# The entry of a transformer block: the first modulation column on TensorE, the root table loaded early, two x tiles scaled by GpSimd

## The chip, the cores and the metric

The kernel runs on one core of a Trainium2 chip. The metric is the device time of one execution in microseconds; the median of three runs of the kernel before is 2016.6 us. The engines of a core are TensorE (PE), VectorE (DVE), ScalarE (ACT), GpSimd (POOL) and SyncE (SP), which here issues nearly all transfers. Each works through its own instructions in order and waits for others on semaphores.

## The reference

One bidirectional encoder block on 512 tokens of 2048 channels. What the change touches is its start:

```
c_act = jax.nn.silu(c)
mod = c_act @ w_ada[l] + b_ada[l]
sh_a, sc_a, gt_a, sh_m, sc_m, gt_m = [m[:, None, :] for m in jnp.split(mod, N_MOD, axis=-1)]
h = rms_norm(x, g_pre_attn[l]) * (1.0 + sc_a) + sh_a
proj = h @ w_in[l]
```

`rms_norm` divides each token by the root of its mean square plus 1e-6 and multiplies by a gain. Then follow two groups of attention heads, an output projection, and a squared-ReLU MLP, all float32.

## The kernel before

**Tiling.** Tokens are in 4 tiles of 128 (`NT`), channels in 16 chunks of 128 (`KD`). Products are made of a high and a low part of each operand, three products each. `x_tok[t]` is a tile of x with tokens on the partitions; `x_t` is x turned, channels on the partitions.

**The entry, per tile t.** ScalarE squares and sums the first 1024 columns (`x_square`, line 843), VectorE the others (line 1514). ScalarE takes the root (`x_root`, line 836), VectorE its reciprocal (line 1520) and scales the tile (`x_scale`, line 1522). TensorE turns the tile in 16 transposes into 4 banks (`turn_x`, line 2369), and ScalarE copies the banks to `x_t` (`x_copies`, line 851).

**Silu and the modulation columns.** silu(c) lies as 16 columns of 128 in `silu_c`. TensorE spreads it over all partitions by 16 transposes into banks 4 to 7 (line 2348, semaphore `spread`), ScalarE copies two of the banks to `silu_b` (line 830), VectorE the other two (line 1475). For chunk n a transposed slice of `w_ada` of 128 x 2048 lands in `w_turned[n % 4]`; `column(n)` on VectorE multiplies it by `silu_b` and sums along the row in one instruction (line 1483), and `column_out(n)` makes of the sum the factor `gsc_a[:, n]` (line 1490). 32 such columns are summed, 16 for the factor and 16 for the shift.

**Heads.** For chunk n ScalarE makes the high part of the weights (`start_w_hi`, line 819) and of h (`start_h`: h_hi and its float32 copy h_f, line 874); VectorE makes the low parts (`start_w_lo`, line 1435; `h_low`, line 1508). TensorE multiplies: chunk 0 in three passes over 7 banks (`first_heads`, lines 2385, 2389, 2393), each later chunk in 21 products (`head_chunk`, lines 2402 to 2404). For n above 4 the low part of h for chunk n - 1 stands on VectorE behind the sum of column n.

**What sets the order.** Each engine's order is written out by hand. SyncE issues gains, ident, bias, x tiles 0 to 2, slice 0, x tile 3, weights 0, and then slice and weights in turn; a buffer is loaded again when its reader has counted up. GpSimd sets `ones` to 1 at the start and has nothing else to do until the end of the 32 columns.

Of the kernel before, what the change touches and what calls it, by code (L numbers as in the profile page):

```python
# [51 lines left out]
X_BANK = (7, 4, 5, 6)  # L52
TURN_BANK = (4, 5, 3, 7)
# [101 lines left out]
def build(nc, a, out, x1_dram, y_dram):  # L155
    with ExitStack() as ctx:
# [29 lines left out]
        scale_b = small("scale_b", [KD])  # L186
        gsc_a = small("gsc_a", [KD])
# [145 lines left out]
        silu_steps, spread, spread_copied = sems("silu_steps spread spread_copied")  # L333
        col_summed, heads_done, heads_out, bias_added = sems("col_summed heads_done heads_out bias_added")

        x_sq, x_var, x_sqrt, x_normed, x_turned, x_t_ready = sems("x_sq x_var x_sqrt x_normed x_turned x_t_ready")
# [475 lines left out]
        def _(act):  # L812
# [15 lines left out]
            for m in range(2):  # L828
                act.wait_ge(spread, m + 1)
                nc.scalar.activation(silu_b[:, m * COLS:(m + 1) * COLS], bank[4 + m][:], ACT.Copy).then_inc(spread_copied, 1)  # L830

            def x_root(t):

                act.wait_ge(x_var, t + 1)
                act.wait_ge(x_sq, t + 1)
                nc.scalar.activation(stat_s[:, t, 0:1], stat[:, t, 0:1], ACT.Sqrt, scale=1.0 / D, bias=stat_v[:, t, 0:1]).then_inc(x_sqrt, 1)

            def x_square(t):

                act.wait_ge(x_landed[t], 16)  # L840
                if t:
                    act.wait_ge(x_sq, t)
                nc.scalar.activation(x_junk[:, 0:HALF], x_tok[t][:, 0:HALF], ACT.Square, accum_out=stat[:, t, 0:1]).then_inc(x_sq, 1)

            def x_copies(t):

                for kk in range(NT):
                    n = NT * t + kk
                    act.wait_ge(x_turned, n + 1)
# [11 lines left out]
            def start_h(n):  # L861

                k = n % KD
                act.wait_ge(cols_ready, n + 1)
                if n >= KD:
                    act.wait_ge(w_used, k + 1)
                else:
                    act.wait_ge(x_t_ready, NT * (NT - 1) + k // 4 + 1)
# [558 lines left out]
        def _(dve):  # L1427
# [45 lines left out]
            for m in (2, 3):  # L1473
                dve.wait_ge(spread, m + 1)
                nc.vector.tensor_copy(silu_b[:, m * COLS:(m + 1) * COLS], bank[4 + m][:]).then_inc(spread_copied, 1)

            def column(n):

                if n == 0:
                    dve.wait_ge(spread_copied, 4)  # L1480
                dve.wait_ge(w_turned_landed[n % RING], 16 * (n // RING + 1))
                w = w_turned[n % RING][:]
                stt(w, w, 1.0, silu_b[:], ALU.mult, ALU.mult, accum_out=col_sum[:, n:n + 1]).then_inc(col_summed, 1)

            def column_out(n):

                k = n % KD
                dve.wait_ge(col_summed, n + 1)
                if n < KD:
                    ts(gsc_a[:, k:k + 1], col_sum[:, n:n + 1], scale_b[:, k:k + 1], gains[:, KD + k:KD + k + 1], ALU.add, ALU.mult).then_inc(cols_ready, 1)  # L1490
                else:
                    tt(shf_a[:, k:k + 1], col_sum[:, n:n + 1], bias[:, k:k + 1], ALU.add).then_inc(cols_ready, 1)
# [17 lines left out]
            def x_square(t):  # L1510

                dve.wait_ge(x_landed[t], 16)
                part_x = x_tok[t][:, HALF:D]
                own.step(stt(x_junk[:, HALF:D], part_x, 1.0, part_x, ALU.mult, ALU.mult, accum_out=stat[:, t, 1:2]))
                ts(stat_v[:, t, 0:1], stat[:, t, 1:2], 1.0 / D, EPS, ALU.mult, ALU.add).then_inc(x_var, 1)

            def x_scale(t):

                dve.wait_ge(x_sqrt, t + 1)
                own.step(nc.vector.reciprocal(rstd[:, t, 0:1], stat_s[:, t, 0:1]))  # L1520
                for cols in (slice(0, COLS), slice(COLS, D)) if t == NT - 1 else (slice(0, D),):
                    ts(x_tok[t][:, cols], x_tok[t][:, cols], rstd[:, t, 0:1], None, ALU.mult).then_inc(x_normed, 1)

            for t in range(NT):
                if t == NT - 1:
                    column(0)
                    column_out(0)
                x_square(t)
                x_scale(t)
            start_w_lo(0)  # L1530
            h_low(0)
            for n in range(1, CHUNKS):
# [3 lines left out]
                column_out(n)  # L1536
                start_w_lo(n)
# [772 lines left out]
        def _(pe):  # L2310
# [31 lines left out]

            pe.wait_ge(const_landed, 32)
            pe.wait_ge(ones_ready, 1)
            pe.wait_ge(silu_steps, 2)
            for k in range(KD):
                b, c = 4 + k // 4, k % 4 * P
                ins = nc.tensor.transpose(bank[b][:, c:c + P], silu_c[:, k:k + 1].broadcast_to([P, P]), ident[:])
                if k % 4 == 3:
                    ins.then_inc(spread, 1)  # L2350

            def turn_x(t):

                for kk in range(NT):
                    n = NT * t + kk
                    if t == NT - 1:
                        b = X_BANK[kk]
                        pe.wait_ge(x_normed, NT + (kk > 0))
                        if kk == 0:
                            pe.wait_ge(spread_copied, 4)  # L2360
                    else:
                        b = kk
                        if t:
                            pe.wait_ge(x_t_ready, n - X_BANKS + 1)
                        else:
                            pe.wait_ge(x_normed, 1)
# [10 lines left out]
            def first_heads():  # L2377
# [3 lines left out]
                for i in range(QH):  # L2381
                    wh, _ = weight_cols(0, i * P)
                    if i >= 4:
                        pe.wait_ge(x_t_ready, KD - NT + i - 2)
# [51 lines left out]
            for t in range(NT):  # L2436
                if t:
                    pe.wait_ge(x_normed, t + 1)
                turn_x(t)
            first_heads()  # L2440
# [676 lines left out]
def packed(a):  # L3117
# [5 lines left out]
    return {"w_ada_t": np.ascontiguousarray(np.concatenate([w_ada[:, SC_A:SC_A + D].T, w_ada[:, SH_A:SH_A + D].T])),  # L3123
# [4 lines left out]
```

## Time and profile before

| what | value |
|---|---|
| median of 3 runs | 2016.6 us (2016.35 to 2017.35) |
| the profiled execution's own time | 2017.13 us |
| its span in the profile | 2015.2 us |
| TensorE busy | 1984.6 us, 98% of the span |
| VectorE busy | 1730.3 us |
| ScalarE busy | 1005.1 us |
| GpSimd busy | 161.3 us |

The profile's times count from the start of the span. The time of an execution is 1.9 us more than its span here. A busy share of a whole run says little about a stage of 50 us; for that one reads the timeline, which lists the instructions in order of time, with the idle time before each in brackets and what ended it.

### The profile page before, as it was taken

To read this page: it belongs to the slowest core of one execution; us is meant where nothing else is said; L and a number is where in the kernel's file an instruction comes from. 1 tells how busy PE (TensorE), PEld (TensorE's weight loads), DVE (VectorE), ACT (ScalarE), POOL (GpSimd) and SP (SyncE) were. 2 spreads that over 40 slices of the span, in tenths; PEclk is the share of its full clock that TensorE was granted. 3 is DMA by queue.
4 is the path that set the end of the run, shared out by engine and by line. 5 is a ranking of instruction groups with operands and counts; after the bars stand their busy time and mean duration, and the time that the engine had idled before them with its cause. 6 is when DMAs were issued, how large, how long until landed. Compare 5 with 4: busy or idle time off the path is not lost.

```text
span 2015.2 us, 30682 instructions
## 1 busy us (share of the span) xinstructions
PE 1984.6 (98%) x11171; PEld 1738.4 (86%) x11171; DVE 1730.3 (86%) x1993; ACT 1005.1 (50%) x1424; POOL 161.3 (8%) x173
## 2 busy tenths in 40 slices
PE   7999999999999999999999999999999999999998
PEld 5887888788888878999999999998888888888886
DVE  7897998788877788999999999988898898898866
ACT  6464223688733374565656565655343343434322
POOL 0000000257400000000000000000300000000000
PEclk9999999999999999999999999999999999999999
DMA  9988768600378746667676766668746546556452
GB/s 357 369 297 293 237 215 233 214 1 21 130 248 261 239 163 188 206 216 230 214 229 213 229 213 229 214 222 331 255 176 250 193 181 250 186 187 252 175 179 84
DMA packets 260180, 432.28 MB, mean 215 GB/s; under 512 B 27648, under 2 KB 155264, under 8 KB 247168
## 3 DMA queue, kind: packets, MB, share of 16 engines
q1 hardware_dynamic: 242576, 361.42, 53.1%
q0 software_dynamic: 15936, 63.97, 8.6%
q10 hardware_dynamic: 1584, 5.77, 0.8%
q8 instruction: 53, 0.87, 0.2%
q14 instruction: 31, 0.25, 0.0%
HBM read 367.15 MB, written 63.96 MB: 214 GB/s over the span
## 4 chain that ended last, share of the span: by engine, by line
PE 91%; DVE 5%; ACT 3%; issue 1%; DMA 0%; POOL 0%; SPq 0%; POOLq 0%; ACTq 0%; DVEq 0%
PE bank L2817 9%; PE bank L2819 9%; PE bank L2818 9%; PE bank L2839 9%; PE bank L2841 9%; PE bank L2840 9%; PE bank L2324 6%; PE bank L2326 6%; PE bank L2325 6%; PE bank L2900 1%; PE bank L2899 1%; PE bank L2898 1%; PE bank L2337 1%; PE bank L2338 1%; PE bank L2339 1%
## 5 line engine op out<-in xcount | busy, mean ns | idle before, releaser
L1367 ACT ACTIVATE hi<-w 128x1024 fp32r<-128x1024 f32 x168 | 178.4, 1062 | 264.8 <-PE bank L2841 197.8
L2839 PE MATMUL bank<-hi,y_use 128*128 128x512 f32 x784 | 306.6, 391 | 0.0
L2840 PE MATMUL bank<-lo,y_use 128*128 128x512 f32 x784 | 305.1, 389 | 0.0
L2841 PE MATMUL bank<-hi,y_use 128*128 128x512 f32 x784 | 305.1, 389 | 0.0
L1286 ACT ACTIVATE hi<-a 128x1024 fp32r<-128x1024 f32 x196 | 206.6, 1054 | 154.5 <-DVE a L2031 141.9
L2028 DVE TENSOR_TENSOR lo<-a,hi 128x1024 fp32r<-128x1024 f32 x196 | 239.1, 1220 | 43.6 <-ACT hi L1286 43.2
L2817 PE MATMUL bank<-h_hi,hi 128*128 128x256 f32 x896 | 253.7, 283 | 0.9 <-DVE c_b L2058 0.9
L2818 PE MATMUL bank<-h_lo,hi 128*128 128x256 f32 x896 | 253.6, 283 | 0.0
L2819 PE MATMUL bank<-h_hi,lo 128*128 128x256 f32 x896 | 253.6, 283 | 0.0
L819 ACT ACTIVATE hi<-raw 128x1024 fp32r<-128x1024 f32 (+2 forms) x120 | 120.5, 1007 | 230.9 <-DMA raw<-in_w_in 66.6
L2143 DVE TENSOR_TENSOR lo<-w,hi 128x1024 fp32r<-128x1024 f32 x168 | 203.9, 1220 | 32.0 <-ACT hi L1367 30.7
L1435 DVE TENSOR_TENSOR lo<-raw,hi 128x1024 fp32r<-128x1024 f32 (+2 forms) x118 | 135.4, 1151 | 51.4 <-ACT hi L819 49.9
L2840 PEld LDWEIGHTS bank<-lo,y_use 128*128 128x128 f32 x784 | 147.2, 188 | 31.4 <-issue 1.0
L2839 PEld LDWEIGHTS bank<-hi,y_use 128*128 128x128 f32 x784 | 147.2, 188 | 31.3 <-issue 1.0
L2841 PEld LDWEIGHTS bank<-hi,y_use 128*128 128x128 f32 x784 | 147.1, 188 | 30.7
L2817 PEld LDWEIGHTS bank<-h_hi,hi 128*128 128x128 f32 x896 | 172.0, 192 | 1.2 <-DVE c_b L2058 1.1
L2818 PEld LDWEIGHTS bank<-h_lo,hi 128*128 128x128 f32 x896 | 172.0, 192 | 0.0
L2819 PEld LDWEIGHTS bank<-h_hi,lo 128*128 128x128 f32 x896 | 172.0, 192 | 0.0
L2031 DVE TENSOR_TENSOR a<-a,a 128x1024 f32<-128x1024 f32 x112 | 134.4, 1221 | 2.0
L2223 DVE TENSOR_TENSOR acc<-bank,acc 128x1024 f32<-128x1024 f32 x84 | 102.3, 1218 | 0.0
L2324 PE MATMUL bank<-hi,h_hi 128*128 128x512 f32 x256 | 100.8, 394 | 0.7 <-DVE lo L1435 0.7
L2326 PE MATMUL bank<-hi,h_lo 128*128 128x512 f32 x256 | 99.7, 389 | 0.0
(402 smaller groups left out, 4700.5 us busy)
## 6 DMA issues: line engine op xcount, KB each, us to landing
w<-in_w_mlp_out SPq DMA_DIRECT2D x128, 512.0 KB, 4.8
a<-in_w_mlp_in SPq DMA_DIRECT2D x112, 512.0 KB, 4.5
y_use<-y_dram SPq DMA_DIRECT2D x53, 1024.0 KB, 9.3
raw<-in_w_ada SPq DMA_DIRECT2D x100, 512.0 KB, 4.7
y_dram<-y_out POOLq DMA_DIRECT2D x28, 1792.0 KB, 6.8
w_turned<-in_w_ada_t SPq DMA_DIRECT2D x32, 1024.0 KB, 7.1
raw<-in_w_out SPq DMA_DIRECT2D x32, 512.0 KB, 4.6
raw<-in_w_heads SPq DMA_DIRECT2D x32, 448.0 KB, 6.5
```

What stands on the lines that cost most here:

```text
L1286: nc.scalar.activation(hi[w.slot()][:], su_weight(i, e)[:].rearrange("p (q k) n -> p q (k n)", q=QROWS), ACT.Copy).then_inc(hi_ready, 1)
L1367: nc.scalar.activation(hi[w.slot()][:], weight(np, i, h)[:], ACT.Copy).then_inc(hi_ready, 1)
L2028: tt(lo[w.slot()][:], src, hi[w.slot()][:].bitcast(F32), ALU.subtract).then_inc(su_lo, 1)
L2143: tt(lo[w.slot()][:], weight(np, i, h)[:], hi[w.slot()][:].bitcast(F32), ALU.subtract).then_inc(dn_lo, 1)
L2324: mm(acc[t][:], xh, hi[s][:, q, :], start=first and q == 0, stop=False)
L2326: ins = mm(acc[t][:], xl, hi[s][:, q, :], start=False, stop=last and q == QROWS - 1)
L2817: mm(into[e], wh, bh, start=opens and k == 0, stop=False, skip_group_check=not opens)
L2818: mm(into[e], wh, bl, start=False, stop=False, skip_group_check=not opens)
L2819: ins = mm(into[e], wl, bh, start=False, stop=k == KH - 1, skip_group_check=not opens)
L2839: mm(bank[b + m][:], yh, hi[s][:, q, :], start=j == 0, stop=False)
L2840: mm(bank[b + m][:], yh, lo[s][:, q, :], start=False, stop=False)
L2841: ins = mm(bank[b + m][:], yl, hi[s][:, q, :], start=False, stop=j == PAIRS - 1)
```

## The change

- TensorE makes 24 products of one column of `ones` before anything else, and 24 transposes of `ident` behind the spreading of silu; both go to bank 0, and nobody reads them (`WARM = 24`).
- ScalarE takes a root of `ones` right after the exponential, which loads the root table there.
- The two engines exchange which banks of silu they copy. The semaphore `spread` becomes the first four counts of `x_turned`.
- VectorE squares tiles 0 and 1 before it takes a reciprocal, and doesn't scale them: GpSimd does. VectorE still scales tiles 2 and 3.
- VectorE copies the turned tile 1 to `x_t`, and ScalarE the other three. ScalarE squares all three first tiles before it copies one, and squares all 2048 columns of tile 3.
- The first column is summed by TensorE, between the turning of tiles 1 and 2: 16 float32 products of one column each, from a slice that the host packs untransposed. `column(0)` on VectorE falls away, and `column_out(0)` reads bank 6.
- `h_low(0)` moves behind `column(1)` and `column_out(1)`.

```diff
@@ scalar
+            act.wait_ge(ones_ready, 1)
+            nc.scalar.activation(stat_s[:, 0, 1:2], ones[:, 0:1], ACT.Sqrt)
-            for m in range(2):
-                act.wait_ge(spread, m + 1)
+            for m in (2, 3):
+                act.wait_ge(x_turned, m + 1)
...
-                act.wait_ge(x_var, t + 1)
+                act.wait_ge(x_dve, (1, 2, 5, 5)[t])
...
+                n = D if t == NT - 1 else HALF
+                nc.scalar.activation(x_junk[:, 0:n], x_tok[t][:, 0:n], ACT.Square, accum_out=stat[:, t, 0:1]).then_inc(x_sq, 1)
...
-            for t in range(NT):
+            for t in range(NT - 1):
                 x_square(t)
                 x_root(t)
-                if t:
-                    if t < NT - 1:
-                        x_copies(t - 1)
-                if t == NT - 2:
-                    x_copies(t)
+            x_copies(0)
+            x_square(NT - 1)
+            x_root(NT - 1)
             start_w_hi(0)
+            x_copies(2)
             x_copies(NT - 1)
@@ vector
-            for m in (2, 3):
-                dve.wait_ge(spread, m + 1)
+            for m in range(2):
+                dve.wait_ge(x_turned, m + 1)
...
-                own.step(nc.vector.reciprocal(rstd[:, t, 0:1], stat_s[:, t, 0:1]))
+                ins = nc.vector.reciprocal(rstd[:, t, 0:1], stat_s[:, t, 0:1])
+                if t < 2:
+                    ins.then_inc(x_dve, 1)
+                    return
+                own.step(ins)
...
-            for t in range(NT):
-                if t == NT - 1:
-                    column(0)
-                    column_out(0)
-                x_square(t)
-                x_scale(t)
+            x_square(0)
+            x_square(1)
+            x_scale(0)
+            x_scale(1)
+            x_square(2)
+            x_scale(2)
+            x_copies(1)
+            column_out(0)
+            x_scale(NT - 1)
             start_w_lo(0)
-            h_low(0)
             for n in range(1, CHUNKS):
                 column(n)
                 if n > RING:
                     h_low(n - 1)
                 column_out(n)
+                if n == 1:
+                    h_low(0)
@@ tensor
+            pe.wait_ge(ones_ready, 1)
+            for _ in range(WARM):
+                mm(bank[0][:, 0:1], ones[:], ones[:, 0:1], start=True, stop=True)
             pe.wait_ge(const_landed, 32)
-            pe.wait_ge(ones_ready, 1)
             pe.wait_ge(silu_steps, 2)
...
+            for _ in range(WARM):
+                nc.tensor.transpose(bank[0][:, 0:P], ident[:], ident[:])
+
+            def first_column():
+
+                pe.wait_ge(spread_copied, 4)
+                pe.wait_ge(w_turned_landed[0], 16)
+                for k in range(KD):
+                    ins = mm(bank[6][:, 0:1], w_turned[0][:, k * P:(k + 1) * P], silu_c[:, k:k + 1], start=k == 0, stop=k == KD - 1)
+                ins.then_inc(col_summed, 1)
...
                 turn_x(t)
+                if t == 1:
+                    first_column()
@@ gpsimd
+            nc.gpsimd.memset(eps[:], EPS)
             nc.gpsimd.memset(ones[:], 1.0).then_inc(ones_ready, 1)
             pool.wait_ge(ones_ready, 1)
+
+            for t in range(2):
+                pool.wait_ge(x_dve, t + 3)
+                nc.gpsimd.tensor_scalar(x_tok[t][:], x_tok[t][:], rstd[:, t, 0:1], None, ALU.mult).then_inc(x_pool, 1)
```

The order of the instructions shows the three places where this moves work. The first is TensorE from its start to the first head product, before; `x_tok_89` to `x_tok_92` are x tiles 0 to 3.

```order
L2348 MATMUL bank<-ident,silu_c 128x128 x16
L2369 MATMUL bank<-ident,x_tok_89 128x128 x16
L2369 MATMUL bank<-ident,x_tok_90 128x128 x16
L2369 MATMUL bank<-ident,x_tok_91 128x128 x16
L2369 MATMUL bank<-ident,x_tok_92 128x128 x16
L2385 MATMUL bank<-h_hi,hi_81 128x512 x7
```

And TensorE in the changed kernel, where `x_tok_90` to `x_tok_93` are x tiles 0 to 3.

```order
L2365 MATMUL bank<-ones 128x1 x24
L2370 MATMUL bank<-ident,silu_c 128x128 x16
L2375 MATMUL bank<-ident 128x128 x24
L2404 MATMUL bank<-ident,x_tok_90 128x128 x16
L2404 MATMUL bank<-ident,x_tok_91 128x128 x16
L2382 MATMUL bank<-silu_c,w_turned_127 128x1 x16
L2404 MATMUL bank<-ident,x_tok_92 128x128 x16
L2404 MATMUL bank<-ident,x_tok_93 128x128 x16
L2420 MATMUL bank<-h_hi,hi_82 128x512 x7
```

The products of `ones` now stand ahead of the spreading, and the first column between tiles 1 and 2.

The second place is VectorE from its copies of silu to the sum of column 1, in the changed kernel.

```order
L1480 COPY silu_b<-bank 128x512 x2
L1519 SCALAR_TENSOR_TENSOR x_junk,stat<-x_tok_90 128x1024
L1520 TENSOR_SCALAR stat_v<-stat 128x1
L1519 SCALAR_TENSOR_TENSOR x_junk,stat<-x_tok_91 128x1024
L1520 TENSOR_SCALAR stat_v<-stat 128x1
L1525 RECIPROCAL rstd<-stat_s 128x1 x2
...
L1538 COPY x_t<-bank 128x4x128 x4
L1495 TENSOR_SCALAR gsc_a<-bank,scale_b,gains 128x1
L1525 RECIPROCAL rstd<-stat_s 128x1
L1531 TENSOR_SCALAR x_tok_93<-x_tok_93,rstd 128x512
L1531 TENSOR_SCALAR x_tok_93<-x_tok_93,rstd 128x1536
L1440 TENSOR_TENSOR lo_86<-raw_76,hi_82 128x896
```

The first reciprocal now stands behind the second square, and `gsc_a` of chunk 0 ahead of the scaling of tile 3 with no sum of a column before it.

The third place is GpSimd. In the kernel before its first tensor-tensor is at line 2961, where an ISA instruction stands ahead of it.

```order
L2925 MEMSET ones 128x128
L2929 MEMSET kr_lo 64x512
L2930 MEMSET kr_lo 64x512
L2960 CAST qr_even<-q_rot 64x512
L2961 ISA
L2961 TENSOR_TENSOR qr_even<-q_rot,qr_even 64x512
```

In the changed kernel GpSimd has the two scalings first.

```order
L2965 MEMSET eps 128x1
L2966 MEMSET ones 128x128
L2971 ISA
L2971 TENSOR_SCALAR x_tok_90<-x_tok_90,rstd 128x2048
L2971 TENSOR_SCALAR x_tok_91<-x_tok_91,rstd 128x2048
L2974 MEMSET kr_lo 64x512
```

The ISA instruction has moved ahead of the first scaling.

## Rows read from the trace of the kernel before

**Rows 1.** The page, part 4: the chain that ended last, shares by engine.
```profile
PE 91%; DVE 5%; ACT 3%; issue 1%; DMA 0%; POOL 0%; SPq 0%; POOLq 0%; ACTq 0%; DVEq 0%
```

**Rows 2.** Waits of TensorE, whole run: us in total, times, longest.
```profile
PE bank L2369 <- DVE x_tok L1522: 9.1, 4, 4.3
PE bank L2348 <- DMA bias<-in_bias_cols: 3.8, 1, 3.8
...
PE bank L2402 <- DVE h_lo L1508: 1.3, 2, 1.0
```

**Rows 3.** Busy time by window: PE, PEld, DVE, ACT, POOL, clock, DMA, GB/s.
```profile
64.00:83.00 19.00, 19.00 (x86) 15.73 (x85) 19.00 (x24) 10.82 (x15) 0.00 (x0) 1.00 0.99 376
```

**Rows 4.** Timeline of the entry: start us, us, engine, line, operation.
```profile
0.88 0.20 POOL L2925 MEMSET ones<- 128x128 f32 x1 [0.29 <-POOLq L3078]
...
3.78 3.65 PE L2348 MATMUL bank<-ident,silu_c 128*128 128x128 f32 x16 [3.78 <-DMA bias<-in_bias_cols]
...
7.29 1.06 ACT L843 ACTIVATE x_junk<-x_tok 128x1024 f32<-128x1024 f32 x1 [0.94 <-DMA x_tok<-in_x]
...
8.52 1.28 ACT L836 ACT_TABLE_LOAD   x1
...
9.81 0.29 ACT L836 ACTIVATE stat_s<-stat,stat_v 128x1 f32<-128x1 f32 x1
...
11.68 5.74 PE L2369 MATMUL bank<-ident,x_tok 128*128 128x128 f32 x32 [4.26 <-DVE x_tok L1522]
...
18.85 2.28 DVE L1483 SCALAR_TENSOR_TENSOR w_turned<-w_turned,silu_b 128x2048 f32<-128x2048 f32 x1
...
23.19 0.16 DVE L1520 RECIPROCAL rstd<-stat_s 128x1 f32<-128x1 f32 x1 [0.42 <-ACT stat_s L836]
...
24.72 1.08 DVE L1435 TENSOR_TENSOR lo<-raw,hi 128x896 fp32r<-128x896 f32 x1
...
25.33 0.72 ACT L874 ACTIVATE h_hi<-x_t,gsc_a 128x512 fp32r<-128x512 f32 x1
...
26.20 2.48 PE L2385 MATMUL bank<-h_hi,hi 128*128 128x512 f32 x7
...
27.31 2.28 DVE L1483 SCALAR_TENSOR_TENSOR w_turned<-w_turned,silu_b 128x2048 f32<-128x2048 f32 x1
...
31.32 0.69 DVE L1508 TENSOR_TENSOR h_lo<-h_f,h_hi 128x512 fp32r<-128x512 f32 x1 [0.41 <-ACT h_f L874]
...
32.16 0.47 PE L2402 MATMUL bank<-h_hi,hi 128*128 128x512 f32 x1 [0.28 <-DVE h_lo L1508]
```

**Rows 5.** Timeline of chunk 4 on VectorE and TensorE.
```profile
46.89 0.69 DVE L1508 TENSOR_TENSOR h_lo<-h_f,h_hi 128x512 fp32r<-128x512 f32 x1
...
47.73 0.47 PE L2402 MATMUL bank<-h_hi,hi 128*128 128x512 f32 x1 [1.03 <-DVE h_lo L1508]
...
50.89 0.69 DVE L1508 TENSOR_TENSOR h_lo<-h_f,h_hi 128x512 fp32r<-128x512 f32 x1
```

**Rows 6.** TensorE: timeline from 15.79; window at 719; line 2616's instructions.
```profile
15.79 1.63 PE L2369 MATMUL bank<-ident,x_tok 128*128 128x128 f32 x13
...
719.00:722.50 3.50, 3.50 (x11) 2.82 (x10) 2.99 (x5) 3.10 (x6) 1.11 (x1) 0.51 0.19 77
...
L2616 PE MATMUL bank<-ones,mod_acc x16: 250/250/271, 406.1 to 407.8; 128*128 128x1 f32 x16
```

**Rows 7.** GpSimd: groups by form, one row of the timeline, line 3030.
```profile
L2949 POOL CAST q_hi<-q_o 128x512 fp32r<-128x512 f32 x14 | 8.5, 610 | 17.7 <-DVE prob L1737 17.6
...
L2988 POOL MEMSET sq_sum<- 128x1024 f32 x1 | 1.0, 961 | 4.2 <-PE bank L2616 4.2
...
390.83 1.30 POOL L2961 TENSOR_TENSOR qr_even<-q_rot,qr_even 64x512 fp32r<-64x512 f32 x1
...
L3030 POOL TENSOR_SCALAR stat_v<-stat x4: 190/190/1114, 703.3 to 720.7; 128x1 f32<-128x1 f32 x4
```

**Rows 8.** Timeline of VectorE and GpSimd side by side.
```profile
393.80 5.50 DVE L1447 SCALAR_TENSOR_TENSOR ga_acc<-raw,silu_c,ga_acc 128x512 f32<-128x512 f32 x4
395.09 0.96 POOL L2968 CAST qr_odd<-qr_round 64x512 fp32r<-64x512 f32 x1
```

More of the change, by code:

```diff
@@ L52 @@
 X_BANK = (7, 4, 5, 6)
+WARM = 24
 TURN_BANK = (4, 5, 3, 7)
@@ L186, in build @@
         scale_b = small("scale_b", [KD])
+        eps = small("eps", [1])
         gsc_a = small("gsc_a", [KD])
@@ L332, in build @@
         gains_landed, const_landed, tab_landed, ones_ready = sems("gains_landed const_landed tab_landed ones_ready")
[L333 removed]
+        silu_steps, x_pool, spread_copied = sems("silu_steps x_pool spread_copied")
         col_summed, heads_done, heads_out, bias_added = sems("col_summed heads_done heads_out bias_added")
[L336 removed]
+        x_sq, x_dve, x_sqrt, x_normed, x_turned, x_t_ready = sems("x_sq x_dve x_sqrt x_normed x_turned x_t_ready")
         mod_summed, mod_reduced, mod_read = sems("mod_summed mod_reduced mod_read")
@@ L1489, in column_out @@
                 if n < KD:
-                    ts(gsc_a[:, k:k + 1], col_sum[:, n:n + 1], scale_b[:, k:k + 1], gains[:, KD + k:KD + k + 1], ALU.add, ALU.mult).then_inc(cols_ready, 1)
+                    ts(gsc_a[:, k:k + 1], bank[6][:, 0:1] if n == 0 else col_sum[:, n:n + 1], scale_b[:, k:k + 1], gains[:, KD + k:KD + k + 1], ALU.add, ALU.mult).then_inc(cols_ready, 1)
                 else:
@@ L1514, in x_square, with x_copies @@
                 own.step(stt(x_junk[:, HALF:D], part_x, 1.0, part_x, ALU.mult, ALU.mult, accum_out=stat[:, t, 1:2]))
-                ts(stat_v[:, t, 0:1], stat[:, t, 1:2], 1.0 / D, EPS, ALU.mult, ALU.add).then_inc(x_var, 1)
+                ts(stat_v[:, t, 0:1], stat[:, t, 1:2], 1.0 / D, EPS, ALU.mult, ALU.add).then_inc(x_dve, 1)
             def x_scale(t):
                 dve.wait_ge(x_sqrt, t + 1)
-                own.step(nc.vector.reciprocal(rstd[:, t, 0:1], stat_s[:, t, 0:1]))
+                ins = nc.vector.reciprocal(rstd[:, t, 0:1], stat_s[:, t, 0:1])
[3 more added lines that the diff above has]
+                own.step(ins)
                 for cols in (slice(0, COLS), slice(COLS, D)) if t == NT - 1 else (slice(0, D),):
                     ts(x_tok[t][:, cols], x_tok[t][:, cols], rstd[:, t, 0:1], None, ALU.mult).then_inc(x_normed, 1)
-            for t in range(NT):
-                if t == NT - 1:
-                    column(0)
-                    column_out(0)
-                x_square(t)
-                x_scale(t)
+            def x_copies(t):
+                for kk in range(NT):
+                    dve.wait_ge(x_turned, NT + NT * t + kk + 1)
+                    src = bank[kk][:].rearrange("p (k n) -> p k n", k=4)
+                    nc.vector.tensor_copy(x_t[:, KD - 4 * kk - 4:KD - 4 * kk, t * P:(t + 1) * P], src).then_inc(x_dve, 1)
+            x_square(0)
[7 more added lines that the diff above has]
+            x_scale(NT - 1)
             start_w_lo(0)
-            h_low(0)
             for n in range(1, CHUNKS):
@@ L2349, in _ @@
                 if k % 4 == 3:
-                    ins.then_inc(spread, 1)
+                    ins.then_inc(x_turned, 1)
+            for _ in range(WARM):
[6 more added lines that the diff above has]
+                ins.then_inc(col_summed, 1)
             def turn_x(t):
@@ L2437, in _ @@
                 if t:
-                    pe.wait_ge(x_normed, t + 1)
+                    if t == 1:
+                        pe.wait_ge(x_pool, 2)
+                    else:
+                        pe.wait_ge(x_normed, t - 1)
                 turn_x(t)
+                if t == 1:
+                    first_column()
             first_heads()
@@ L3122, in packed @@
     columns = lambda *rows: np.ascontiguousarray(np.concatenate([r.reshape(-1, P) for r in rows]).T)
-    return {"w_ada_t": np.ascontiguousarray(np.concatenate([w_ada[:, SC_A:SC_A + D].T, w_ada[:, SH_A:SH_A + D].T])),
+    first = w_ada[:, SC_A:SC_A + P].reshape(KD, P, P).transpose(1, 0, 2).reshape(P, D)
+    return {"w_ada_t": np.ascontiguousarray(np.concatenate([first, w_ada[:, SC_A + P:SC_A + D].T, w_ada[:, SH_A:SH_A + D].T])),
             "w_heads": np.ascontiguousarray(np.concatenate([head(h) for h in EARLY], axis=1)),
```

25 lines of the change are left out of this document (13 added, 12 removed).

## The prediction

> **What bounds the kernel now.** I read the chain that ended last first: it is TensorE nine tenths of the way [rows 1], so only time that TensorE stands still, or runs at half rate, can be gained or lost. The waits of TensorE over the whole run [rows 2] give the size of the stake: 9.1 us before the transposes of x, 3.8 before silu is spread, 1.3 before head products. From 64 to 83 us TensorE is busy all the time [rows 3], and the units behind it are paced by TensorE's own releases. So a shift of TensorE's work at about 48 us should reach the end of the kernel undiminished, and a change before that is worth what it moves that point.
>
> The timeline of the entry [rows 4] has the chain. TensorE spreads silu(c) from 3.78 on, ScalarE squares the first x tile from 7.29, loads the root table at 8.52 and takes the root at 9.81; VectorE scales the tile, and TensorE turns it from 11.68. VectorE sums column 0 for 2.28 us from 18.85. The first h_hi is made at 25.33, the first head product starts at 26.20, chunk 1 at 32.16. At chunk 4 TensorE waits 1.03 us once more, for an h_lo which stands on VectorE behind the sum of column 5 [rows 5]; from there on VectorE makes an h_lo every 4.0 us (46.89 to 50.89), and TensorE took 4.85 us a chunk before (three from 32.16 to 46.70), so chunk 4 is the point at which the entry's delay is settled. VectorE starts column 1 at 27.31 and has hardly a break from there.
>
> **TensorE's rate.** The transposes from 11.68 start every 0.216 us at first (19 of 32 before 15.79), then 13 of them take 1.63 us, about 0.113 apart [rows 4, 6]. The clock column shows 1.00 in both stretches, but it does show 0.51 at 719 us, and products there take twice as long [rows 6]; I read the first 4.1 us of that burst as the 1.2 GHz level. A single fp32 product of one column is two records of TensorE: eight products of line 2616 are 16 records, 0.113 us apart at the full clock [rows 6].
>
> **The change, step by step** (times of the profiled execution).
>
> *24 products before silu is spread.* 48 records from about 1.2 us (the memset of ones ends at 1.08, and one more small memset stands before it). At the full clock 48 x 0.113 = 5.4 us, end at 6.6; at half clock 48 x 0.216 = 10.4, end at 11.6. I take a rise after 4.3 us of work, as in the burst at 11.68: 20 records, then 28 x 0.113, end at 8.7. The spread started at 3.78, so it is 4.9 us late. It runs at the full clock then, and its third and fourth bank come at 10.2 and 10.7. VectorE's and ScalarE's copies of it stand ahead of their squares in order, which is the cost of this part: ScalarE's first square starts at 11.35 in place of 7.29.
>
> *Root table ahead.* ScalarE loads it (1.28 us [rows 4]) while it waits for the spread. First square to first root becomes 1.25 us and was 2.5, so the root is ready at 12.9 and was at 10.1: 2.8 us late.
>
> *GpSimd scales tiles 0 and 1.* The reciprocal of tile 0 now stands behind VectorE's second square (half of column 0's 2.28 us in length, so about 1.2 with 0.3 of small ones), so GpSimd starts at 13.8. The trace has no such operation. Nearest: a cast of 512 columns takes 0.61 us, a memset of 1024 columns 0.96, a tensor-tensor of 512 columns 1.29 [rows 7]. Four casts would be 2.44 us for a tile, twice the memset 1.92, four tensor-tensors 5.2. Added to it: the first of four equal small scalar operations takes 1.11 us, the others 0.19 [rows 7], so 0.9 once; and where VectorE works on SBUF beside it a cast goes from 0.61 to 0.96 us, while four products of VectorE of 512 columns take 5.50, 1.4 each, where one of 2048 columns takes 2.28 alone [rows 4, 8]. VectorE squares tile 2 and scales it in this time. I take 5.8 us for the two tiles (2 x 1.95, 0.9, and about 0.5 each for the sharing), with bounds 3.9 (the memset's rate, nothing added) and 10.4. Tile 1 is ready at 19.6.
>
> The Trainium skill, GPSIMD Engine Reference, section 3.1 has 1.03 cycles an element for the simplest bodies, which at its 1.2 GHz is an estimate of 1.76 us for a tile; by it the two tiles would take about 0.4 us less than in my sum. Its section 1 says that GpSimd shares its SBUF interfaces with VectorE, and by that rule the trace agrees.
>
> *TensorE.* Turning tile 0 fits between. Tile 1 is turned from 19.7 to 21.5 (16 x 0.113). Then the first column: 16 fp32 products of one column, 32 records x 0.113 = 3.6 us, in TensorE's order ahead of tiles 2 and 3. Its input had landed before 18.85, when VectorE read it, and is no bound. It ends at 25.15. On VectorE it took 2.28 us and gave gsc_a at 21.1; now gsc_a starts at 25.3. VectorE's copies of tile 1, four of 512 columns, lie beside it and cost nothing; without that cover they would be some 2.5 us. The second 24 transposes (2.8 us) end at 13.3, before tile 0 is scaled, and cost nothing.
>
> *From there on.* VectorE: gsc_a 0.2, then the reciprocal, the scaling of tile 3 and the low part of the first weights, which took from 23.19 to 25.80 before: the sum of column 1 starts at 28.1 and did at 27.31. ScalarE squares all of tile 3 alone (1.9 us), beside first column. TensorE turns tile 2 from 25.15 to 27.0 and the first bank of tile 3 until 27.6; ScalarE's copy and then h_hi at 28.4, which was at 25.33; the first head product at 29.3, 3.1 us late. The 7-product passes take as long as before and end 2.8 us late, since the short wait for h_lo before 32.16 is gone: chunk 1 starts at 35.0. ScalarE makes the next h 3.6 to 4.6 us after its first; h_low of chunk 0 stands now behind the sum of column 1, and h_lo of chunk 1 starts at 33.4 in place of 31.32, 2.1 us late. VectorE and ScalarE keep their pace to chunk 4, whose h_lo is then ready 2.1 us late as well. TensorE would be free for it 2.8 us later than it was (46.7), so its wait shrinks from 1.03 to 0.3 and chunk 4 starts at 49.8, where it was 47.73.
>
> Sum: +2.1 us. The profiled execution took 2017.13 us with a span of 2015.2; it should become 2019.2 and 2017.3. Against the median of 2016.6 that is 2018.7. Within 0.2% of it (4.0 us) is about what a measurement can't tell from no change.
>
> **The rivals.**
>
> *The entry is no slower, or a little quicker.* The clock may be at the full rate soon after 1.2 us (start of the squares 2.1 us earlier), and GpSimd may take 3.9 for its two tiles (1.9 less). Either alone gives about 2016.7, both 2014.7. For it speaks that no row shows the level before 3.78; against it, that the burst at 3.78 was at half rate all its 3.65 us. Chance 0.20, for -4 to +0.5 us.
>
> *GpSimd becomes the bound (the other side).* At 10.4 us for the two tiles, the rate of its tensor-tensors, first column, gsc_a and h_hi all come 4.6 us later: +6.7, 2023.3. It decides from 7.7 us for the two tiles on. For it speaks how both engines stretch in [rows 8]; against it, that only one input is a tile. Chance 0.14.
>
> *Code for GpSimd.* The order shows an ISA instruction ahead of the first scaling, which stood ahead of the first tensor-tensor in the kernel before; there the operation started 0.09 us after the cast before it and took its usual 1.30 [rows 7], so nothing was paid. If the first scaling did pay as much as would take the two tiles beyond 7.7 us, the result is that of the rival above: 2021 and more. Chance 0.03. The Trainium skill, GPSIMD Engine Reference, section 2.1 has about 6 us for the first call of freshly loaded code; by that rule the time would be about 2024, and the trace does not agree at the one place where it could.
>
> *Faster by over 0.2%.* If products of one column cost next to nothing, the spread keeps its place, gsc_a comes at 19.4, and chunk 4 starts at 43.6: 2012.5. The row of 0.113 speaks against it. Chance 0.05.
>
> The forecast itself, +0.5 to +4 us, has 0.58. It takes in that TensorE, idle from 13.3 to 17.1, falls to the lower clock for turning tiles 0 and 1: 1.3 us more, 2020.0. In [rows 2] its longest idle time before a transpose of x was 4.3 us, and the work behind it ran at half rate.
>
> **Numbers.** Over 4.0 us slower: 0.14 + 0.03 = 0.17. Faster: 0.05. Same: 0.20 + 0.58 = 0.78. The range runs from both quick bounds together, 2014.7, to where a tenth or so is left above, 2022.0.
>
> **What would show it.** The first 24 products end near 8.7 and ScalarE's first square starts near 11.4; a square at 7.3 refutes the first term. GpSimd's scalings take 2.4 to 3.5 us each. The 32 records of the first column take 3.6 us and start near 21.5. h_hi near 28.4, chunk 4 near 49.8 with a wait well under 1.03 us. The prediction is wrong if TensorE's waits behind 60 us differ from before, if GpSimd needs over 3.9 us a tile, or if the one-column products are far from 0.113 us.

## The result, and the profile after

The changed kernel takes 2029.91 us (median of 6 runs, 2028.09 to 2032.18), the kernel before 2016.47 (6 runs): a ratio of 1.0064, 95% interval 1.0054 to 1.0075. It is 13.4 us slower. The forecast was 2018.7, with 2014.7 to 2022.0 as its range: the result lies 7.9 us beyond the range.

The profiled execution took 2028.09 us with a span of 2026.1. Its timeline of the entry stands against [rows 4] (start, length, engine, line, operation, and in brackets the idle time before and what ended it):

```profile
1.17 10.40 PE L2365 MATMUL bank<-ones 128*128 128x1 f32 x48 [1.17 <-POOL ones L2966]
...
11.43 3.65 PE L2370 MATMUL bank<-ident,silu_c 128*128 128x128 f32 x16
...
14.88 3.67 PE L2375 MATMUL bank<-ident 128*128 128x128 f32 x24
...
15.62 1.05 ACT L848 ACTIVATE x_junk<-x_tok 128x1024 f32<-128x1024 f32 x1
...
17.54 10.88 POOL L2971 TENSOR_SCALAR x_tok<-x_tok,rstd 128x2048 f32<-128x2048 f32 x2 [16.43 <-DVE rstd L1525]
...
18.69 3.64 DVE L1519 SCALAR_TENSOR_TENSOR x_junk<-x_tok 128x1024 f32<-128x1024 f32 x1
...
23.04 3.27 PE L2404 MATMUL bank<-ident,x_tok 128*128 128x128 f32 x16 [4.49 <-POOL x_tok L2971]
23.09 6.42 DVE L1531 TENSOR_SCALAR x_tok<-x_tok,rstd 128x2048 f32<-128x2048 f32 x1
...
28.48 1.97 PE L2404 MATMUL bank<-ident,x_tok 128*128 128x128 f32 x16 [2.17 <-POOL x_tok L2971]
...
30.28 3.66 PE L2382 MATMUL bank<-silu_c,w_turned 128*128 128x1 f32 x32
...
33.81 5.32 PE L2404 MATMUL bank<-ident,x_tok 128*128 128x128 f32 x32
...
33.98 0.28 DVE L1495 TENSOR_SCALAR gsc_a<-bank,scale_b,gains 128x1 f32<-128x1 f32 x1 [2.09 <-PE bank L2382]
...
38.62 0.72 ACT L880 ACTIVATE h_hi<-x_t,gsc_a 128x512 fp32r<-128x512 f32 x1
...
59.91 0.47 PE L2437 MATMUL bank<-h_hi,hi 128*128 128x512 f32 x1 [0.46 <-DVE h_lo L1513]
```

Read down TensorE's rows. The products of ones run until 11.57, so the spread of silu starts at 11.43 and not at 3.78. TensorE then waits for GpSimd, twice. The first head product starts at 39.48, right behind the h_hi of 38.62, in place of 26.20, and chunk 4, the last row, starts at 59.91 where it started at 47.73 [rows 5]: 12.2 us late. In these two executions that is the whole loss, and a little more. TensorE's waits over the whole run (us in total, times, longest) stand against [rows 2]: the longest is GpSimd's, and of the waits behind the entry only one is new, 0.7 us for `comb`.

```profile
PE bank L2404 <- POOL x_tok L2971: 6.7, 2, 4.5
...
PE bank L2365 <- POOL ones L2966: 1.2, 1, 1.2
...
PE bank L2344 <- DVE comb L1894: 0.7, 1, 0.7
...
PE bank L2437 <- DVE h_lo L1513: 0.5, 1, 0.5
```

The two spans differ by 10.9 us, 1.3 less than the 12.2. The profiled execution of before has a wait of 1.6 us at its line 2337 with no releaser; after has none there. Seven of the executions below show 0.2 to 1.5 us at the same product, the others none. I found no cause for it. With it, the new wait for `comb` (0.7) and a wait for `z_tok` that is 0.3 shorter (1.2 and 1.5), the difference behind chunk 4 is accounted for: 12.2 - 1.6 + 0.7 - 0.3 is 11.0.

The clock column by window (the columns are those of [rows 3]; the clock is the third from the end):

```profile
1.20:11.40 10.20, 10.20 (x48) 10.20 (x49) 0.77 (x4) 2.66 (x4) 0.00 (x0) 1.00 0.86 314
15.00:18.50 3.50, 3.50 (x25) 3.31 (x23) 1.86 (x7) 3.19 (x8) 0.96 (x1) 1.00 1.01 419
23.00:26.40 3.40, 3.27 (x16) 2.87 (x16) 3.37 (x2) 1.85 (x4) 3.40 (x1) 0.57 1.03 422
...
30.30:33.90 3.60, 3.60 (x35) 3.60 (x34) 1.59 (x3) 0.00 (x0) 0.00 (x0) 0.98 0.00 0
33.90:39.00 5.10, 5.10 (x33) 4.98 (x32) 4.97 (x7) 3.27 (x6) 0.00 (x0) 0.68 0.79 270
```

The column says 1.00 from 1.20 to 11.40 too, where the records are 0.216 us apart, nearly twice what the prediction's rows have at the full clock; so its 1.00 is no proof of the full clock ahead of the first fall that it shows, and the spacing of the records has to be read beside it. By the spacing TensorE is at 1.2 GHz until some way into the second 24 transposes and at 2.4 GHz before it waits for GpSimd (the microsecond from 17 on holds 12 of them, the one from 14 on 7 records). It is near 1.2 GHz for the turning of tile 0 behind the wait, at the full clock again for tile 1 and the first column, and at the low level for about half of the turning of tiles 2 and 3 (0.50 from 34 to 37 us, 1.00 from 37.5 on). I had priced one such fall, at 1.3 us.

### The profile page after: what moved, and what is told of

Read it like the earlier page. It is cut to its first block, busy times and chain, and to the rows that moved or that the text cites. A ratio compares the mean times of both kernels' runs of the same rounds, so it can differ in the third digit from the quotient of the medians.

```text
span 2026.1 us, 30901 instructions
## 1 busy us (share of the span) xinstructions
PE 2002.2 (99%) x11275; PEld 1756.5 (87%) x11275; DVE 1733.9 (86%) x1990; ACT 1004.6 (50%) x1421; POOL 170.4 (8%) x176
## 4 chain that ended last, share of the span: by engine, by line
PE 89%; DVE 5%; ACT 3%; issue 1%; DMA 1%; POOL 1%; DVEq 0%; ACTq 0%; POOLq 0%
PE bank L2857 9%; PE bank L2859 9%; PE bank L2858 9%; PE bank L2880 9%; PE bank L2879 9%; PE bank L2881 9%; PE bank L2344 5%; PE bank L2346 5%; PE bank L2345 5%; PE bank L2940 1%; PE bank L2938 1%; PE bank L2939 1%; PE bank L2357 1%; PE bank L2359 1%; PE bank L2358 1%
```

## The experiments

Two suspects were left by the timeline: the 24 products ahead of the spread, and the scaling on GpSimd. The first three kernels ran together, each with 10 runs beside 25 of the kernel before (2016.65). The edits are against the changed kernel unless another is named; they are shown cut, with "..." where lines are left out, and the waits that move with an edit are mostly not shown.

**The products left out.**
```diff
-            for _ in range(WARM):
-                mm(bank[0][:, 0:1], ones[:], ones[:, 0:1], start=True, stop=True)
```


> The changed kernel without the 24 one-column products at the start; all else as changed. Theory: they hold back the spreading of silu by 10.4 us at half clock, and cost what ScalarE's and VectorE's first squares lose, about 5.7 us at the reciprocal of tile 0 (17.2 becomes 11.5, since the second x tile has to land first), so the run is 5 to 6.5 us shorter than the changed kernel, some 2024. GpSimd still takes 5.4 us for each tile. Rival: GpSimd's scaling alone sets the entry and the products cost nothing beside it: the time stays at 2030 within 1 us.

Measured 2023.29 (2021.66 to 2027.09), ratio 1.0029 [1.0019, 1.0038]: 6.6 us less than the changed kernel. The spread is back at 3.78.

**The scaling back on VectorE, the products kept.**
```diff
+                own.step(ins)
                 if t < 2:
-                    ins.then_inc(x_dve, 1)
+                    ts(x_tok[t][:], x_tok[t][:], rstd[:, t, 0:1], None, ALU.mult).then_inc(x_dve, 1)
                     return
...
-            for t in range(2):
-                pool.wait_ge(x_dve, t + 3)
-                nc.gpsimd.tensor_scalar(x_tok[t][:], x_tok[t][:], rstd[:, t, 0:1], None, ALU.mult).then_inc(x_pool, 1)
```


> The changed kernel with tiles 0 and 1 scaled by VectorE again (GpSimd scales nothing); the 24 products stay. Theory: turning tile 1 starts at about 20.5 in place of 28.5, VectorE's square of tile 2 is back at 1.2 us and its scaling at 1.3 (3.6 and 6.4 with GpSimd at work), the run is 7 to 8.5 us shorter than the changed kernel, some 2022. Rival: the turning of tiles 0 and 1 is set by VectorE's order anyway, so that VectorE's extra 2.6 us eat most of it: less than 4 us shorter.

Measured 2021.55 (2019.87 to 2023.36), ratio 1.0022 [1.0013, 1.0032]: 8.4 us less than the changed kernel, with chunk 4 at 52.36.

**Both undone** (the two edits together; the early root table, the second 24 transposes, the squares' order and the first column on TensorE stay).

> Both edits at once: no one-column products at the start and VectorE scales all tiles. Theory: the two costs add up, since they lie one behind the other in the chain: 13 to 16 us shorter than the changed kernel, 2014 to 2017, that is the kernel before or up to 3 us less. Rival: with both gone the first column on TensorE (3.7 us between two tiles) is the next bound and leaves the kernel 2 us or more slower than the kernel before.

Measured 2015.73 (2012.84 to 2021.20), ratio 0.9991 [0.9981, 1.0002]: no slower than before. So the two parts hold the whole loss. The steps between the four medians are 5.8 (products, on VectorE's scaling), 7.6 (scaling, without products), and 14.2 for both at once; 5.8 and 7.6 make 13.4. So each part costs nearly the same with the other there as without it (5.8 and 6.6 for the products, 7.6 and 8.4 for the scaling). From the timeline of this kernel:

```profile
7.22 4.06 PE L2373 MATMUL bank<-ident 128*128 128x128 f32 x24
...
12.90 1.97 PE L2402 MATMUL bank<-ident,x_tok 128*128 128x128 f32 x16 [1.62 <-DVE x_tok L1528]
...
16.53 2.02 PE L2402 MATMUL bank<-ident,x_tok 128*128 128x128 f32 x16 [1.66 <-ACT x_t L856]
...
18.39 3.63 PE L2380 MATMUL bank<-silu_c,w_turned 128*128 128x1 f32 x32
...
21.88 3.69 PE L2402 MATMUL bank<-ident,x_tok 128*128 128x128 f32 x32
```

TensorE never stands for more than 1.7 us here between the transposes and the column, and every turning is at the full clock: 32 transposes behind the column take 3.69 us, and 5.32 in the changed kernel.

**GpSimd by itself.** Ahead of the rest, with VectorE and ScalarE held back until it is done, GpSimd fills a scratch tile, scales it in three ways and copies half of it. The scratch work is extra, and nothing reads it.
```diff
+            act.wait_ge(x_pool, 1)
...
+            dve.wait_ge(x_pool, 1)
...
+            own.step(nc.gpsimd.memset(x_junk[:], 1.0))
+            own.step(nc.gpsimd.tensor_scalar(x_junk[:], x_junk[:], ones[:, 0:1], None, ALU.mult))
+            own.step(nc.gpsimd.tensor_scalar(x_junk[:, 0:HALF], x_junk[:, 0:HALF], ones[:, 0:1], None, ALU.mult))
+            own.step(nc.gpsimd.tensor_scalar(x_junk[:, 0:HALF], x_junk[:, 0:HALF], 1.0, None, ALU.mult))
+            nc.gpsimd.tensor_copy(x_junk[:, 0:HALF], x_junk[:, HALF:D]).then_inc(x_pool, 1)
```


> The changed kernel with five operations of GpSimd put ahead of the squares, on a scratch tile, while VectorE has nothing to do: a memset of 2048 columns, scalings by a column of 2048 and of 1024 columns, a scaling by a constant of 1024, a copy of 1024. Theory: GpSimd's scaling is slow by itself: 5.4 us for 2048 and 2.7 for 1024 columns with VectorE idle. Rival: sharing with VectorE doubled it: alone 2048 columns take about 2.4 us. The time of the whole run only shows the delay of some 10 us and tells nothing else.

Its one run took 2032.47 us, with chunk 4 at 65.28. Its timeline, GpSimd first alone and then in its usual place beside VectorE:

```profile
1.17 1.81 POOL L2971 MEMSET x_junk<- 128x2048 f32 x1
3.07 5.45 POOL L2972 TENSOR_SCALAR x_junk<-x_junk,ones 128x2048 f32<-128x2048 f32 x1
8.62 2.85 POOL L2973 TENSOR_SCALAR x_junk<-x_junk,ones 128x1024 f32<-128x1024 f32 x1
11.55 2.77 POOL L2974 TENSOR_SCALAR x_junk<-x_junk 128x1024 f32<-128x1024 f32 x1
14.39 1.04 POOL L2975 COPY x_junk<-x_junk 128x1024 f32<-128x1024 f32 x1
...
16.80 1.22 DVE L1520 SCALAR_TENSOR_TENSOR x_junk<-x_tok 128x1024 f32<-128x1024 f32 x1
...
18.38 10.86 POOL L2978 TENSOR_SCALAR x_tok<-x_tok,rstd 128x2048 f32<-128x2048 f32 x2 [2.96 <-DVE rstd L1526]
...
18.75 4.41 DVE L1520 SCALAR_TENSOR_TENSOR x_junk<-x_tok 128x1024 f32<-128x1024 f32 x1
...
23.93 6.40 DVE L1532 TENSOR_SCALAR x_tok<-x_tok,rstd 128x2048 f32<-128x2048 f32 x1
```

A tile costs GpSimd 5.45 us when nothing runs beside it and 5.43 when VectorE does. So neither sharing nor a first call is in the price: it is the rate of the operation, 2.7 times that of a copy of the same 1024 columns. A scale given as a constant is hardly cheaper (2.77 against 2.85). The sharing falls on VectorE alone: its square of 1024 columns goes from 1.22 to 4.41 us, and its scaling from 1.29 (with both undone) to 6.40. That scaling ends at 30.33, 1.1 us behind GpSimd's end at 29.24: it stood nearly all that time. The square was over at 23.16, some 0.6 us before GpSimd's first tile (23.8, with half of 10.86 for a tile), so by these rows it was slowed, but not held to the end of GpSimd's instruction.

**The first column on VectorE again**, with both suspects undone (column(0) ahead of column_out(0) on VectorE; the products of first_column are gone).
```diff
             x_copies(1)
+            column(0)
             column_out(0)
```


> As the run with both undone, and the first column is summed by VectorE again, at the place where it now waits for TensorE's sum (between its copies of tile 1 and the scaling of tile 3); the slice is packed transposed again. Theory: TensorE loses 3.6 us between tiles 1 and 2 in that run, and VectorE waits there 2.25 us, so VectorE's 2.28 us fit into its wait: the first h_hi comes about 0.8 us earlier than with the column on TensorE (24.4 in place of 25.2), chunk 4 up to 0.8 us earlier; a gain under 1 us, not to be told apart in the medians. Rival: the first column on TensorE does spare VectorE time that counts, and this run is 2 us or more slower than the one with both undone.

Measured 2013.98 (11 runs, 2013.26 to 2017.99), ratio 0.9988 [0.9978, 0.9997]. Its gsc_a comes at 22.21 and h_hi at 24.64, where both undone has 22.06 and 25.22. From its timeline:

```profile
19.89 2.29 DVE L1488 SCALAR_TENSOR_TENSOR w_turned<-w_turned,silu_b 128x2048 f32<-128x2048 f32 x1
...
23.18 0.70 PE L2395 MATMUL bank<-ident,x_tok 128*128 128x128 f32 x4 [2.50 <-DVE x_tok L1531]
```

Tiles 1 and 2 are turned by 20.7 without TensorE's 3.63 us for the column. Most of VectorE's 2.29 us comes behind that, and TensorE stands 2.50 us until tile 3, which VectorE scales behind its sum, is ready. On balance chunk 4 starts at 46.03 in place of 46.52. The median is the lowest of all, 1.8 us under both undone, but the two ran in different sets, and their ratios to the kernel before are 0.9988 and 0.9991 with intervals that overlap: which of the two is faster isn't shown. Against the kernel before it gains 0.12%: the interval just leaves out no change, and the gain is less than the 0.2% named in the prediction.

**The products 128 columns wide**, in the changed kernel: the same 48 records, more columns in each.
```diff
-                mm(bank[0][:, 0:1], ones[:], ones[:, 0:1], start=True, stop=True)
+                mm(bank[0][:, 0:P], ones[:], ones[:], start=True, stop=True)
```


> The changed kernel with the 24 products at the start made 128 columns wide in place of one; the same 48 records. Theory: products of one column don't raise TensorE's clock, wide ones do: the 48 records start 0.216 us apart and go on at the full clock after some 4 us, so they end between 7 and 9 us and not at 11.57, and silu is spread at the full clock (16 transposes in 1.9 us and not 3.65). Rival: the clock can't rise this early whatever TensorE does, and the block ends at 11.5 us again.

One run: 2027.29.

```profile
1.17 7.45 PE L2365 MATMUL bank<-ones 128*128 128x128 f32 x48 [1.17 <-POOL ones L2966]
...
8.46 1.91 PE L2370 MATMUL bank<-ident,silu_c 128*128 128x128 f32 x16
...
18.88 3.52 PE L2404 MATMUL bank<-ident,x_tok 128*128 128x128 f32 x16 [5.89 <-POOL x_tok L2971]
...
26.68 6.83 PE L2382 MATMUL bank<-silu_c,w_turned 128*128 128x1 f32 x32
```

128 columns a product are over sooner than one column a product: 7.45 us against 10.40, since the clock rises within them, and the spread behind them is at the full clock (1.91, not 3.65), so GpSimd starts at 13.38 and not at 17.54. This is what I had assumed of the narrow ones: an end at 8.7, and it is 8.62. But the gain was lost again. GpSimd is the same 10.88 us, and behind the 5.89 us of waiting the clock is down; the first column takes 6.83 us at 1.2 GHz in place of 3.66, tiles 2 and 3 take 6.52 in place of 5.32, and chunk 4 starts at 59.91 as in the changed kernel. That is one execution of each: as executions of one kernel differ by such steps (below), what wide products are worth at the median isn't shown.

**The second 24 transposes left out**, with both suspects undone.
```diff
-            for _ in range(WARM):
-                nc.tensor.transpose(bank[0][:, 0:P], ident[:], ident[:])
```


> As the run with both undone, without the second 24 transposes too. Theory: they raise the clock before tile 0 is turned; without them tile 0 is turned at the lower clock (3.6 us in place of 1.97 at 12.9) and perhaps tile 1, and the 32 records of the first column, which don't raise it, may take up to 6.9 us: 1 to 6 us longer than with them. Rival: nothing waits for tile 0's turning that long (ScalarE's copies start at 15.8), so within 0.5 us.

Measured 2015.63 (2013.66 to 2018.45), ratio 0.9996 [0.9986, 1.0005], against 2015.73 with them. Tiles 0 and 1 are turned in 5.65 us from 12.69, some 20 of their 32 transposes at the low clock (an estimate from 0.216 and 0.113 us each), and not in 1.97 and 2.02; but with them the second turning stood 1.66 us waiting for ScalarE's copies, and chunk 4 starts at 46.30 without them, at 46.52 with them. In this kernel they are worth nothing.

**The kernel before, with the early root table and the 24 transposes alone.**
```diff
+            act.wait_ge(ones_ready, 1)
+            nc.scalar.activation(stat_s[:, 0, 1:2], ones[:, 0:1], ACT.Sqrt)
...
+            for _ in range(24):
+                nc.tensor.transpose(bank[0][:, 0:P], ident[:], ident[:])
```


> The kernel before with two parts of the change alone: the root table loaded right after the exponential, and the 24 transposes behind the spreading of silu. Theory: tile 0 is scaled about 1.2 us earlier (10.34 becomes 9.1), tile 1 after its landing; the transposes of tile 0 run at the full clock; all later steps of the entry come 0.5 to 1.2 us earlier, and the run is about 1 us shorter than the kernel before, which the medians hardly show. Rival: the third and fourth x tile and the weights land too late for any gain: within 0.3 us at chunk 4.

Measured 2014.89 (11 runs, 2014.69 to 2018.38), ratio 0.9992 [0.9983, 1.0001]. h_hi starts at 24.20 and chunk 4 at 46.59, 1.1 us earlier than [rows 4, 5] have them; the total can't tell it from no change. Which of the two parts gives it was not run apart.

**The same kernels again.** The profiled execution of the kernel without products had been the slowest of its ten, with chunk 4 only 1.0 us ahead of the changed kernel's, while the medians are 6.6 apart. So it was profiled twice more, and the changed kernel once.

> The kernel without the first 24 products again, for a second profiled execution. The first one profiled was the slowest of ten (2027.09 us, median 2023.29) and has TensorE at half rate through the first column (6.8 us) and the turns. Theory: the executions of this kernel differ by when the clock comes back in the entry; an execution near 2023 shows the first column in 3.6 us and the turns of tiles 2 and 3 in about 3.7, and chunk 4 starts near 54 to 56 us in place of 58.87. Rival: they differ behind the entry; then chunk 4 starts near 58.9 again whatever the time.

> The same kernel a third time, for a third profiled execution. Theory: the time of the execution less the start of chunk 4 is the same in all three within 1 us (it was 2027.09 - 58.87 = 1968.2). Rival: that difference takes up the spread of 5 us between executions, and chunk 4 starts at one place.

> The changed kernel again. Its profiled execution was the fastest of six (2028.09, median 2029.91). Theory: an execution near 2030 has one more stretch at half rate in the entry than the first (the second turn, 1.97 us, or the first column, 3.66 us, takes up to twice as long), and chunk 4 starts near 61.5; GpSimd's two tiles take 10.9 us as before. Rival: chunk 4 starts near 59.9 again, and the rest differs.

They took 2025.35, 2022.70 and 2030.14 us. The turning of tile 1 and the first column in the three executions without products, first the slowest:

```profile
22.89 3.67 PE L2402 MATMUL bank<-ident,x_tok 128*128 128x128 f32 x16 [1.76 <-POOL x_tok L2969]
...
26.36 6.82 PE L2380 MATMUL bank<-silu_c,w_turned 128*128 128x1 f32 x32
...
58.87 0.47 PE L2435 MATMUL bank<-h_hi,hi 128*128 128x512 f32 x1 [0.49 <-DVE h_lo L1513]
```

then the second,

```profile
23.25 3.35 PE L2402 MATMUL bank<-ident,x_tok 128*128 128x128 f32 x16 [1.76 <-POOL x_tok L2969]
...
26.44 3.99 PE L2380 MATMUL bank<-silu_c,w_turned 128*128 128x1 f32 x32
...
56.83 0.47 PE L2435 MATMUL bank<-h_hi,hi 128*128 128x512 f32 x1 [0.47 <-DVE h_lo L1513]
```

and the third,

```profile
22.52 3.56 PE L2402 MATMUL bank<-ident,x_tok 128*128 128x128 f32 x16 [1.76 <-POOL x_tok L2969]
...
25.92 3.79 PE L2380 MATMUL bank<-silu_c,w_turned 128*128 128x1 f32 x32
...
55.54 0.47 PE L2435 MATMUL bank<-h_hi,hi 128*128 128x512 f32 x1 [0.46 <-DVE h_lo L1513]
```

The same program waits the same time for GpSimd ahead of tile 1 (1.76 us) and has its clock back in time for the column in two of three executions. Tiles 2 and 3, expected in about 3.7 us where the column is fast, took 6.65 and 5.19 there: the clock fell again. The time less the start of chunk 4 is 1968.2, 1968.5 and 1967.2 us, 1.4 us apart at most where I had expected 1, while chunk 4 itself is up to 3.3 us apart. In the thirteen profiled executions of this study that show a wait ahead of chunk 4, those of before and after among them, it lies between 1966.9 and 1969.4, though chunk 4 moves from 46.3 to 65.3. So the spread between these three executions lies mostly in the entry, and there mostly in the clock: of the 3.3 us between the first and the third, 3.0 are the column. The Trainium skill, TensorE: Matmul & The Clock Gate, Part 1, warns of this too: how many products run cold differs from run to run of one kernel. The changed kernel's second execution also bears it out: tile 1 is turned in 3.61 us and not 1.97, and chunk 4 starts at 61.39.

**The first column ahead of the turning of tile 1**, with both suspects undone.
```diff
             for t in range(NT):
+                if t == 1:
+                    first_column()
                 if t:
...
-                if t == 1:
-                    first_column()
```


> The kernel with both suspects undone (2015.73 us, chunk 4 at 46.52), with the first column's products ahead of the turning of tile 1 in place of behind it, so that they fill 1.66 us in which TensorE waited for ScalarE's copies of tile 0. Theory (the column's cost is its place in TensorE's order): it starts near 14.9, gsc_a comes near 18.7 in place of 22.06, turning tile 3 near 22.3 and h_hi near 24.2, chunk 4 at 45.5 to 46.0, so about 0.8 us less: 2014.9. Rival (VectorE's order sets it: its copies of tile 1, then the scaling of tile 3, come later, as the turning of tile 1 does): no gain, chunk 4 at 46.5 or later and 2015.7. If the column's input lands later than 14.9, TensorE waits for it and it is slower.

Measured 2015.34 (11 runs, 2012.94 to 2019.13), ratio 0.9992 [0.9983, 1.0001]; both undone has 2015.73. The theory missed. From the timeline:

```profile
16.24 3.93 PE L2380 MATMUL bank<-silu_c,w_turned 128*128 128x1 f32 x32
...
24.12 0.27 DVE L1495 TENSOR_SCALAR gsc_a<-bank,scale_b,gains 128x1 f32<-128x1 f32 x1
```

The column is over at 20.2, and yet gsc_a comes 2.1 us later than with both undone: it stands on VectorE behind the copies of tile 1, and tile 1 is turned from 20.04 now, where it was from 16.53. Chunk 4 starts at 48.09, 1.6 us later than with both undone; the medians don't show the 1.6, and in this execution the time less that start is 1966.9, the lowest of all. No gain is what the rival, VectorE's order, had said. But in this execution tile 0 was turned in 3.36 us and not in 1.97, which is the clock and puts the column 1.3 us behind the 14.9 of the theory. How much of the 1.6 us is VectorE's order and how much the clock isn't separated.

## Why the prediction was wrong

**The place of the loss** was right: the entry, settled at chunk 4, with the rest passed on whole. It forecast chunk 4 at 49.8; it is 59.91. Nearly all of the 10.1 us between them is three terms.

**"I take a rise after 4.3 us of work": failed.** The 48 records of the first 24 products are 0.216 us apart to the last, end at 11.57 and not 8.7, and leave the clock down for the spread behind them. I had carried the rise over from 128-column transposes to one-column products. The upper bound of the term (11.6) was there, but the sum went by the middle, and the spread at half rate was no part of the bound. ScalarE's first square is at 15.62 and not 11.35, 4.3 us late. The table was early as forecast. VectorE's second square was over before the root was there and cost nothing, where I had it hold the reciprocal back, so GpSimd's scaling starts at 17.54 and not 13.8: 3.7 us.

**"I take 5.8 us for the two tiles ... with bounds 3.9 and 10.4": failed.** They took 10.88, beyond the upper bound: 5.1 us. The rival "GpSimd becomes the bound" (0.14) is what happened; it was priced for 10.4 us, and the two other terms came on top. I set the price by the casts and the memset, on the ground that only one input is a tile. The rows that were nearest were the tensor-tensors, 1.30 us for 512 columns [rows 7], 5.2 for a tile; 5.44 was measured. Both additions to the price were wrong as well: no first-call cost showed (5.45 for the first, 5.43 and 5.44 for the two of the change), and VectorE beside it added nothing. The Trainium skill, GPSIMD Engine Reference, section 3.1 gave the 1.76 us a tile that I quoted as an estimate; the measurement decides against it here, by a factor of three. What section 1 of the same page of the Trainium skill says of interfaces shared with VectorE, the trace bears out on VectorE's side (1.22 to 3.64 us, 1.28 to 6.42). Of the 6 us that its section 2.1 has for freshly loaded code nothing is seen: the first scaling of the change took no longer than the second.

**"Turning tile 1 and the first column": right.** 1.97 us and 3.66, forecast 1.8 and 3.6, in the profiled execution. That both are at the full clock there is the luck of that execution.

**The clock behind the wait.** I had one fall, 1.3 us, for the turning of tiles 0 and 1. It did come at tile 0, hidden behind GpSimd's second scaling. The costly one I did not have: about half of the transposes of tiles 2 and 3 at half rate, 5.32 us for the 32 where both undone has 3.69. h_hi is 10.2 us behind its forecast where gsc_a is 8.7 behind, so that is 1.5 us. What brings the clock down there is not settled. The column runs at the full clock in both kernels, and with both undone the clock holds behind it; there TensorE had stood 1.7 us at the most between its transposes before it, and here 4.5 and 2.2. The length of the waits alone doesn't decide it: without the second 24 transposes TensorE had stood 4.64 us ahead of tile 0, and the 32 transposes behind the column still took 3.69; with the column ahead of tile 1 it had stood 3.33, and the clock fell behind the column (0.57 from 20 to 22 us).

**"Its wait shrinks from 1.03 to 0.3"**: it is 0.46, right but for 0.2.

**No cost for the second 24 transposes**: right, and no gain either with both suspects undone. **The early root table**: added to the kernel before together with those transposes, it starts chunk 4 1.1 us earlier.

In sum 3.7 + 5.1 + 1.5 is 10.3 us, and 10.1 were missed at chunk 4; smaller steps, each off by 0.1 or 0.2, make up the rest.

## What to carry to other kernels

Price an operation on GpSimd by a row of the same operation or of its nearest neighbour in kind; a cast or a memset is no stand-in for arithmetic, and a range built from them will not reach it. Work moved to GpSimd to free VectorE can hold up VectorE for most of that time (here two instructions of VectorE grew by 7.6 us while GpSimd worked for 10.9), so count both engines' time, and what TensorE's clock does while it waits for them. Before work is put on TensorE only to keep its clock up, look whether just that form of work raises it: here 24 narrow products ran at half rate to the end and held up the spread by 7.7 us.

## What the runs showed of the hardware

- One-column fp32 products back to back did not bring the clock up: 48 records in 10.40 us, against 7.45 for 48 records of 128 columns, in the same place.
- A clock that is down can stay down through such products (6.82 us for 32 records in one execution without the first 24, 6.83 with them made wide) or come back at their start (3.99 and 3.79 in two more executions without the first 24), and one that is up can hold (3.63 us).
- GpSimd's tensor-by-scalar of 128x2048 f32 takes 5.45 us, of 128x1024 2.85; a copy of 128x1024 takes 1.04, a memset of 128x2048 1.81.
- Beside it VectorE's scaling of one tile goes from 1.29 to 6.40 us, its square of 1024 columns from 1.22 to 4.41, and GpSimd's scaling does not change (5.45 and 5.43).
- Three executions of one kernel, with the same wait of 1.76 us for GpSimd ahead of tile 1, had chunk 4 at 55.5, 56.8 and 58.9 us, mostly by when the clock came back in the entry and fell again.
- The clock column of the windows read 1.00 over 10.2 us in which TensorE's records were 0.216 us apart; the spacing of records showed the level there.
